# Block inverse in the scans: 64 of 128 columns formed at each doubling level, packed in PSUM

## What is computed

```python
def run_gdn(q, k, v, g, beta, s0, emit):
    q, k, v, g, beta = map(to_chunks, (q, k, v, g, beta))
    lower = jnp.tril(jnp.ones((CHUNK, CHUNK), dtype=bool))
    strict = jnp.tril(jnp.ones((CHUNK, CHUNK), dtype=bool), -1)
    gc = jnp.cumsum(g, axis=-1)
    decay = jnp.exp(jnp.where(lower, gc[..., :, None] - gc[..., None, :], -jnp.inf))
    kb = k * beta[..., None]
    lmat = jnp.where(strict, jnp.einsum('bhncd,bhnsd->bhncs', kb, k) * decay, 0.0) + jnp.eye(CHUNK, dtype=k.dtype)
    rhs = jnp.concatenate([v * beta[..., None], kb * jnp.exp(gc)[..., None]], axis=-1)
    sol = lax.linalg.triangular_solve(lmat, rhs, left_side=True, lower=True, unit_diagonal=True)
    ...
    def step(s, inp):
        u = u0_i - jnp.einsum('bhcd,bhde->bhce', kcd_i, s)
        s_new = s * gl_i[..., None, None] + jnp.einsum('bhcd,bhce->bhde', kd_i, u)
        ...
```

## Time and profile before

| | us |
|---|---|
| median of 3 runs | 4242.95 (4242.53 to 4243.0) |
| profiled execution | 4243.44 |
| its span, first to last instruction | 4241.6 |
| mean granted clock of TensorE | 0.965 |
| the scans | 332 to 738 of the span |

### The profile page before, as it was taken

The page is one execution under the profiler, slowest core; times in us unless marked ns, Lnnn a source line. Parts: engine busy times, 40 slices in busy tenths (PEclk is TensorE's granted clock), DMA queues, the critical chain, the costliest instruction groups (busy, mean ns, idle before and its releaser), DMA issues.

```text
span 4241.6 us, 47935 instructions
## 1 busy us (share of the span) xinstructions
PE 4000.2 (94%) x19804; PEld 3293.7 (78%) x19804; DVE 2067.0 (49%) x3065; ACT 1285.8 (30%) x1860; POOL 454.2 (11%) x513
## 2 busy tenths in 40 slices
PE   7898899999998998999999998999999999999997
PEld 4677889778877886788888875888778878778886
DVE  5535656655546764433443454433453443454345
ACT  2314423332232222322322236322332223243223
POOL 1005453000001111000300014000000000000001
PEclk8998999899999998999999999999999999999999
DMA  5220000544431110322323211223232222112322
GB/s 185 79 71 14 1 1 12 171 137 152 139 114 57 39 48 30 119 90 94 105 85 108 86 55 53 90 90 102 81 110 89 96 84 92 39 46 87 107 80 75
DMA packets 344099, 351.28 MB, mean 83 GB/s; under 512 B 9547, under 2 KB 340107, under 8 KB 343628
## 3 DMA queue, kind: packets, MB, share of 16 engines
q1 hardware_dynamic: 343884, 348.22, 25.5%
HBM read 345.83 MB, written 2.10 MB: 82 GB/s over the span
## 4 chain that ended last, share of the span: by engine, by line
PE 87%; DVE 6%; ACT 3%; issue 2%; DMA 1%; POOL 0%; SPq 0%; POOLq 0%; DVEq 0%; ACTq 0%
PE ps L370 22%; PE ps L371 22%; PE ps L372 22%; PE ps L1436 5%; PE ps L2299 3%; PE ps L2290 1%; ACT whi L346 1%; DVE wlo L352 1%; PE ps L3170 1%; DVE macc L949 1%; PE ps L457 1%; PE ps L459 1%; PE ps L458 1%; DMA raw<-in_ab_w_in 1%; PE ps L3157 1%
## 5 line engine op out<-in xcount | busy, mean ns | idle before, releaser
L352 DVE TENSOR_TENSOR wlo<-raw,whi 128x2048 fp32r<-128x2048 f32 (+4 forms) x316 | 629.6, 1993 | 1132.0 <-ACT whi L346 1132.0
L370 PE MATMUL ps<-Xh,whi 128*128 128x512 f32 x2640 | 1042.0, 395 | 19.5 <-DVE Xl L510 7.6
L371 PE MATMUL ps<-Xl,whi 128*128 128x512 f32 x2640 | 1034.1, 392 | 0.0
L372 PE MATMUL ps<-Xh,wlo 128*128 128x512 f32 x2640 | 1033.8, 392 | 0.0
L346 ACT ACTIVATE whi<-raw 128x2048 fp32r<-128x2048 f32 (+4 forms) x316 | 523.7, 1657 | 1214.7 <-PE ps L372 1090.1
L370 PEld LDWEIGHTS ps<-Xh,whi 128*128 128x128 f32 x2640 | 499.3, 189 | 132.4 <-issue 25.6
L371 PEld LDWEIGHTS ps<-Xl,whi 128*128 128x128 f32 x2640 | 499.5, 189 | 106.0 <-issue 1.7
L372 PEld LDWEIGHTS ps<-Xh,wlo 128*128 128x128 f32 x2640 | 498.7, 189 | 106.5 <-issue 0.3
L370 PE MATMUL ps<-HDh,whi 128*128 128x512 f32 x1056 | 411.7, 390 | 0.0
L372 PE MATMUL ps<-HDh,wlo 128*128 128x512 f32 x1056 | 410.9, 389 | 0.0
L371 PE MATMUL ps<-HDl,whi 128*128 128x512 f32 x1056 | 410.8, 389 | 0.0
(11 more groups left out here) (547 smaller groups left out, 5656.8 us busy)
## 6 DMA issues: line engine op xcount, KB each, us to landing
raw<-in_ffn_w SPq DMA_DIRECT2D x44, 1024.0 KB, 5.4
raw<-in_ffa_w_gate_up SPq DMA_DIRECT2D x44, 1024.0 KB, 5.0
raw<-in_ffb_w_gate_up SPq DMA_DIRECT2D x44, 1024.0 KB, 5.0
mslot<-in_mod_w SPq DMA_DIRECT2D x28, 1024.0 KB, 7.9
raw<-in_mod_w SPq DMA_DIRECT2D x20, 1024.0 KB, 7.8
raw<-in_ab_w_in SPq DMA_DIRECT2D x14, 1024.0 KB, 5.2
raw<-in_ffn_w SPq DMA_DIRECT2D x16, 768.0 KB, 4.3
raw<-in_hy_w_in SPq DMA_DIRECT2D x12, 1024.0 KB, 5.1
```

What stands on the lines that cost most here:

```text
L352: dve.tensor_tensor(k.part(k.wlo, c), k.raw(c), k.part(k.whi, c).bitcast(F32), ALU.subtract).then_inc(*k.ev.put("dve_wlo", ("lo", n), ("ra ...
L370: pe.matmul(o, wh, xh, start=first, stop=False)
L371: pe.matmul(o, wh, xl, start=False, stop=False)
L372: return pe.matmul(o, wl, xh, start=False, stop=last)
```

## The change

At level `part`, X and XT are block diagonal and B has one quarter of each pair of blocks, so B X has values only in every other run of b columns, and the same holds for both products that are subtracted. `level(x, part, w)` picks those columns out of a tile (runs of b, every second one, w says which), and `packed` gives the matching view of a contiguous piece. Now
- each matmul of `BT` and `XP` has a moving operand of 64 columns and writes 64 contiguous columns of its bank: 128 columns for two heads in `BT`, 256 for `XP`;
- ScalarE writes 128 columns of Pm instead of 256;
- VectorE subtracts in two instructions of 128 columns, X first and then XT, each with its own event, and then zeroes the 128 columns of Pm that the next level does not write, since Pm is also a stationary operand and counts with all its columns;
- TensorE waits for XT and, between the two halves of `XP`, for that zeroing ("P zero");
- two memsets of 128 x 512 in the preparation zero Pm once.

The order of the steps and `TURNS` stay. The number of TensorE instructions stays.

```diff
--- before.py
+++ after.py
@@ -1361,6 +1361,18 @@
     return x.unsqueeze(2).to_broadcast([128, 2, 128])
 
 
+def level(x, part, w):
+
+    s = 2 << part
+    if len(x.shape) == 3:
+        x = x.rearrange("p a c -> p (a c)")
+    return x.rearrange("p (b w c) -> p b w c", w=2, c=s)[:, :, w, :]
+
+
+def packed(x, part):
+    return x.rearrange("p (b c) -> p b c", c=2 << part)
+
+
 def two_heads(hp):
     return 2 * hp, slice(2 * hp, 2 * hp + 2)
 
@@ -1455,15 +1467,23 @@
         ps = bank("BT")
         pe.wait_ge(*ev.at(("BT",) + me))
         pe.wait_ge(*ev.at(("X",) + me))
-        both(ps, lambda hh: k.BT[:, d, h0 + hh], lambda hh: X[:, hh]).then_inc(*put(sig, ("mm", "BT") + me))
+        for hh in range(2):
+            ins = pe.matmul(packed(ps[:, hh * 64:hh * 64 + 64], part), k.BT[:, d, h0 + hh], level(X[:, hh], part, d), start=True,
+                            stop=True)
+        ins.then_inc(*put(sig, ("mm", "BT") + me))
     elif s == "XP":
         pe.wait_ge(*ev.at(("P",) + me))
-        if part == 0:
-            pe.wait_ge(*ev.at(("XT", d, hp, j)))
+        pe.wait_ge(*ev.at(("XT", d, hp, j, part)))
         ps = bank("X")
         if part < 4:
-            both(ps, lambda hh: XT[:, hh], lambda hh: k.Pm[:, d, h0 + hh])
-        both(ps[:, 256:512], lambda hh: k.Pm[:, d, h0 + hh], lambda hh: XT[:, hh]).then_inc(*put(sig, ("mm", "X") + me))
+            for hh in range(2):
+                pe.matmul(packed(ps[:, hh * 64:hh * 64 + 64], part), XT[:, hh], level(k.Pm[:, d, h0 + hh], part, d), start=True,
+                          stop=True)
+        pe.wait_ge(*ev.at(("P zero", d, part) + ((hp, j) if (j, part) != (0, 0) else ())))
+        for hh in range(2):
+            ins = pe.matmul(packed(ps[:, 128 + hh * 64:192 + hh * 64], part), k.Pm[:, d, h0 + hh], level(XT[:, hh], part, 1 - d),
+                            start=True, stop=True)
+        ins.then_inc(*put(sig, ("mm", "X") + me))
     elif s == "kt":
         ps = bank("kt")
         for hh in range(2):
@@ -1471,7 +1491,7 @@
         ins.then_inc(*put(sig, ("mm", "kt") + me))
     elif s == "u0":
         ps = bank("u0")
-        pe.wait_ge(*ev.at(("X", d, hp, j, 5)))
+        pe.wait_ge(*ev.at(("XT", d, hp, j, 5)))
         pe.wait_ge(*ev.at(("kb",) + me))
         both(ps, lambda hh: XT[:, hh], lambda hh: k.N_[:, d, h0 + hh])
         both(ps[:, 256:512], lambda hh: k.NT[:, d, h0 + hh], lambda hh: XT[:, hh]).then_inc(*put(sig, ("mm", "u0") + me))
@@ -1622,7 +1642,8 @@
         act.wait_ge(*ev.at(("mm", "BT") + me))
         if part > 0:
             act.wait_ge(*ev.at(("mm", "X", d, hp, j, part - 1)))
-        act.activation(k.Pm[:, d, hs], b2(ps("BT")), ACT.Copy).then_inc(*put(sig, ("P",) + me, ("out", "BT") + me))
+        act.activation(level(k.Pm[:, d, hs], part, d), packed(ps("BT")[:, 0:128], part), ACT.Copy).then_inc(
+            *put(sig, ("P",) + me, ("out", "BT") + me))
     elif s == "kc":
         act.wait_ge(*ev.at(("mm", "u0") + me))
         act.activation(k.UK[d][hp][:, :, :, :], ps("u0")[:, :].rearrange("p (b a c) -> p b a c", b=2, a=2), ACT.Copy).then_inc(
@@ -1669,6 +1690,8 @@
     dve.memset(k.atEO[1][:, :, :], 0.0)
     dve.memset(k.SL[0][:, :, :, :], 0.0).then_inc(*ev.put("dve_prep", "SL zero"))
     dve.memset(k.SG[0][:, :, :, :], 0.0).then_inc(*ev.put("dve_prep", "SG zero"))
+    for d in range(2):
+        dve.memset(k.Pm[:, d, :, :], 0.0).then_inc(*ev.put("dve_prep", ("P zero", d, 0)))
     dve.wait_ge(*ev.at(("mm", "gab cols")))
     pv = k.bk.of(("gab cols",))[:, 0:96].rearrange("p (t c) -> p t c", t=6)
     dve.tensor_tensor(k.gx[:, :, :], pv[:, :, 0:8], k.col("dtb", 0, 8).unsqueeze(1).to_broadcast([128, 6, 8]),
@@ -1734,10 +1757,16 @@
             *put(sig, ("at",) + me, ("out", "at") + me))
     elif s == "Xn":
         dve.wait_ge(*mm("X"))
-        o = XX[:, :, :, :] if part < 4 else XX[:, 1:2, :, :]
-        x = ps("X")[:, :].rearrange("p (b a c) -> p b a c", b=2, a=2)
-        dve.tensor_tensor(o, o, x if part < 4 else x[:, 1:2], ALU.subtract).then_inc(
-            *put(sig, ("X", d, hp, j, part + 1), ("out", "X") + me))
+        x = ps("X")
+        if part < 4:
+            o = level(XX[:, 0], part, d)
+            dve.tensor_tensor(o, o, packed(x[:, 0:128], part), ALU.subtract).then_inc(*put(sig, ("X", d, hp, j, part + 1)))
+        o = level(XX[:, 1], part, 1 - d)
+        dve.tensor_tensor(o, o, packed(x[:, 128:256], part), ALU.subtract).then_inc(
+            *put(sig, ("XT", d, hp, j, part + 1), ("out", "X") + me))
+        if (j, part) != (5, 4):
+            nj, npart = (j, part + 1) if part < 4 else (j + 1, 0)
+            dve.memset(level(k.Pm[:, d, hs], npart, 1 - d), 0.0).then_inc(*put(sig, ("P zero", d, npart, hp, nj)))
     elif s == "kt":
         dve.wait_ge(*mm("kt"))
         dve.tensor_tensor(k.N_[:, d, hs], k.vtok[:, t, hs], by2(bd), ALU.mult)
@@ -1868,7 +1897,7 @@
         pool.wait_ge(*ev.at(("NT",) + me))
         pool.tensor_tensor(XT, k.NT[:, d, hs], over2(k.Ums[:, 9 - d, :]), ALU.mult).then_inc(*put(sig))
         pool.wait_ge(*ev.now())
-        pool.tensor_tensor(XT, XT, over2(k.ident[:, :]), ALU.add).then_inc(*put(sig, ("XT", d, hp, j)))
+        pool.tensor_tensor(XT, XT, over2(k.ident[:, :]), ALU.add).then_inc(*put(sig, ("XT", d, hp, j, 0)))
     elif s == "BT":
         if part > 0:
             pool.wait_ge(*ev.at(("mm", "BT", d, hp, j, part - 1)))
```

## The result

| | before | after |
|---|---|---|
| median, us | 4242.98 (4242.53 to 4246.1, 4 runs) | 4276.1 (4274.61 to 4278.45, 4 runs) |
| ratio to before, 95% interval | | 1.0077 (1.0066 to 1.0089) |
| profiled execution, its span | 4243.44, 4241.6 | 4277.39, 4275.6 |
| mean granted clock of TensorE | 0.965 | 0.953 |
| first `BT` matmul of the levels, us from the start | 342.72 | 343.03 |

The changed kernel is 33 us slower, and all of it lies in the scans. The view of busy time by stretch shows where. Columns: the stretch in us, its length, busy us and number of instructions of each engine, granted clock of TensorE, DMA share, GB/s.

What follows compares the result with a forecast made beforehand. TensorE was taken to bound the scans, busy 369.6 of 406.0 us. Terms 1 - 3 + 23.2 + 12.2 = +33.4 us on 4242.95 gave 4276; range 4236 to 4320, the forecast's own 4252 to 4292.

Steps and rivals of the forecast that it cites:

- Part 1: TensorE's 1344 level passes in the scans: weight load sets the pace, so halving moving columns gains 0 us.
- the third rival (C): Level passes shorten with their columns, -75 us, giving 4168; chance 0.01.
- Part 2: Each level's chain: smaller P copy and split subtraction make X ready some 0.35 us sooner, -3 us (0 to -11).
- Part 3: Zeroing: 116 memsets add VectorE work but 0 on the path; two preparation memsets add +1 us (0 to 1.3).
- Part 4: TensorE's clock in the scans: narrow passes keep it at 0.50 through two stretches, +23.2 and +12.2 us.
- The first: Stretch 349.1 to 375.0 us: 231 passes stay at half clock, 49.1 us replacing 25.9, +23.2 us.
- The second: Stretch 618.8 to 640.0 us: 157 passes stay at half clock, 33.4 us replacing 21.2, +12.2 us.
- the second rival (B): Scans' clock falls more often and stays low longer; one or two further stretches give 4299 to 4322; chance 0.18.
- A's: Rival in which the clock does not mind pass width: 4241 us (4233 to 4244); chance 0.28.

Runs made afterwards that it cites:

- e1: Changed kernel with TensorE's level matmuls 128 columns wide again into an unpacked bank, ScalarE and VectorE as changed: 4235.93 us, ratio 0.999.
- e12: The same kernel as e1, run later on another chip: 4237.33 us, ratio 0.999.
- e2: Kernel before plus 116 memsets of 128 columns of a spare tile behind VectorE's subtractions: 4243.99 us, ratio 0.9995.
- e3: Changed kernel with level matmuls 64 wide only in token tiles j = 0 and 1, 128 wide from j = 2 on: 4241.43 us, ratio 1.0014.
- e9: e1 with 48 useless 128-wide matmuls put into two long TensorE waits (20 and 28 passes): 4240.26 us, ratio 0.9993.
- e4: Changed kernel with level matmuls 128 wide at j = 0 and 1, 64 wide from j = 2 on: 4257.52 us, ratio 1.004.
- e8: Changed kernel with the first head of each pair 64 wide, the second 128, in all level products (672 narrow passes): 4255.09 us, ratio 1.003.
- e10: Changed kernel with the same useless matmuls as e9 in the same two waits: 4274.4 us, ratio 1.0085.
- e6: Changed kernel with only the BT matmuls 64 wide (480 narrow passes), XP 128 wide: 4236.89 us, ratio 0.9985.
- e7: The changed kernel unaltered, run once more on another chip: 4273.68 us, ratio 1.0071 to the kernel before.

## Why the prediction was right, and where it was not

The time, 4276 forecast and 4276.1 measured, agrees to a degree that its terms don't. That the loss comes from narrow passes at half clock was foreseen and is shown; that it comes to the forecast's number is luck.

- **Part 1, passes.** Right. 194 passes in 20.80 us at 1.00, 160 of them 64 wide, are 0.107 us each; 188 in 41.00 us at 0.50 are 0.218. Halving the columns gave no throughput; the third rival (C) did not come. The Trainium skill, "TensorE: Matmul & The Clock Gate", section "LDWEIGHTS (loading the stationary operand)", gives columns / 1.2 ns, an estimate of 107 ns for 128. The row at 1.00 agrees; at 0.50 it is twice that. The rule that the prediction takes for C from the section "Back-to-back issue gap" of this page of the Trainium skill stands there for a matmul by itself; the same section says that in a stream of weight loads and matmuls the spacing is set by both, with which the rows agree.
- **Part 2, the chain.** -3 forecast, -3.4 measured in the scans (e1 and e12 against before), which fits but lies near the spread of the profiles with wide passes (392.3 to 397.3).
- **Part 3, zeroing.** Right for the path: e2 measures the memsets at nothing, and no wait of TensorE ends with one. The size of VectorE's work was wrong, and wrong in sign. The forecast added the lengths of the instructions, 5 to 18 us more. They do add up to 33.3 + 27.2 + 19.1 = 79.6 us where the one took 65.7 + 10.0 (96 x 684 and 24 x 415 ns), but they overlap, and VectorE is busy 8.5 us less in the scans. The sum did not use this. The first `BT` matmul starts 0.3 us later, for 1 forecast, but it starts anywhere from 341.3 to 347.1 us in the profiles, so this term is not measured.
- **Part 4, the clock.** That narrow passes keep the clock down was right, and e1 shows it, but the step that laid out the stretches failed. The first was put at 49.1 us more at 0.50 and +23.2. In the changed kernel's own time that is up to 398 us; the 375 in the forecast's last paragraph is where this work ends in the kernel before and doesn't fit its sum. It ended at 355.2, 6.9 us more than before and, at 0.4, about +3. In the profiled execution of e3 it came as forecast, 269 passes in 58.0 us for 255 (24 + 231) in 55.9. The second was put at 33.4 us more and +12.2: it was 44 us more (58.0 for 13.7), about +18. The new one of 41 us, about +16, was not foreseen at all. Together there are 94 us more at 0.50 than before, for 49.1 + 33.4 = 82.5 forecast, and each cost 0.39 us and not the 0.43 of the forecast (35.4 / 82.5): 37 us for 35.4. That is why the sum holds. Its first term was mis-sized by a factor of eight, and an event of the second rival (B), a further stretch, took its place.
- **The step behind that.** The forecast took narrow passes as unable to bring the clock back, and the stretch as ending where wide ones come. That the clock could fall at a new place was only in rival B: the forecast took TensorE's waits from the trace of before and counted as dangerous only those behind which the clock already fell. The SB wait that ends at 469.38 us had left it at 1.00 there. Whether narrow passes or the place of the wait against the clock's last change made it fall in the changed kernel is open; e9 shows new falls with wide passes alone.
- **The test at its end** was wrong too: "if the clock is 1.00 behind 350 us, the time is A's". It was 1.00 behind 355.2, and the time was not A's. A clock term needs the whole stage as its test, not one place; the mean of the scans (under 0.90 forecast, 0.84) was the one that told.
- **What stays open.** Why the first stretch ends at 355 us in both profiles of the changed kernel and lasts 58 us in e3, where the same passes are narrow until 404; what picks the kind of an execution of e3, e4, e8 and e10; behind which waits the clock falls; and whether it is the number of moving columns or their short runs that keeps it down. The Trainium skill, "TensorE: Matmul & The Clock Gate", section "What's actually happening", says that the chip sets the clock by how busy TensorE has been and that the number of matmuls at the low clock varies from run to run. The second agrees with e3, whose executions take 4240 or 4265 us. Of the first, the rows show that it is not busy time as the profile counts it: 41.00 of 41.00 us busy, and the clock stayed at 0.50.

## What to carry to other kernels

Before making matmuls narrower, look at what sets the pace of a pass: where the weight load does, as here (0.107 to 0.112 us a pass at either width), fewer moving columns buy nothing and can cost the clock. Judge that cost over all of TensorE's waits in the stage, also those behind which the clock stands now, at some 0.4 us for each further microsecond at half clock, and take several executions, since one kernel can have two kinds. What was narrowed on the other engines could be kept: e1 and e6, wide or mostly wide on TensorE and small on ScalarE and VectorE, were the fastest kernels here, some 6 to 7 us by their medians (0.15%, at the edge of what can be told) below before, about half of it behind the scans.

## What the runs showed of the hardware that I had not expected

- Behind the same wait of 1.44 us, with the same 21 passes and 1.96 us busy around it, the clock went to 0.50 in both profiles of the changed kernel and stayed at 1.00 in e1, e12 and e8. With wide passes it fell a little earlier in the work in e9, behind a wait of 1.75 us.
- 160 narrow passes of 194, with no wait between them, left the clock at 1.00 for 20.8 us; 188 passes without a break, 88 of them narrow level work, did not bring it back for 41 us.
- Against e6 (4236.89 us) on the same chip, half of the level passes narrow cost 18 us (e8, from 4240 to 4273) and all of them 37 (e7, 4273.68).
- One kernel, e3, runs at 4240 or at 4265 us, with 58 us at 0.50 in the one long execution that has a trace; another, the changed one, stays within 6.3 us (4272.18 to 4278.45).
- Filling two waits with matmuls of no use removed the stretches behind them, others came, and nothing was gained.
- VectorE and ScalarE take 128 columns in runs of 2 to 32 at 278 to 284 ns; VectorE's instructions of this kind overlap.
